# A two-layer mixer block and a gated block on one core: the opening, the start of layer 1 and the ends of layers re-ordered

## What is computed

```python
for l in range(2):
    mod = silu(c) @ w_ada[l] + b_ada[l]            # 3 x 1024: shift, scale, gate
    h = rms_norm(x, norm_g[l]) * (1.0 + scale) + shift
    proj = h @ w_in[l]                             # gq, gk, gv, glr, gz, dq, dk, dv, dz
    gqkv = silu(causal_depthwise_conv([gq, gk, gv], conv_w[l]))
    o_gla = gla_branch(...)                        # chunked gated linear attention, gate of rank 16
    o_diff = diff_branch(...)                      # block-causal attention; q and k normed by heads
    x = x + gate * ([o_gla, o_diff] @ w_out[l])
```

## Time and profile before

| | us |
|---|---|
| median of three runs | 1829.73 |
| lowest, highest | 1824.44, 1832.11 |
| the profiled execution's own time | 1827.28 |
| its span, from the first to the last instruction | 1825.5 |

### The profile page before, as it was taken

The page is one execution under the profiler, slowest core; times in us unless marked ns, Lnnn a source line. Parts: engine busy times, 40 slices in busy tenths (PEclk is TensorE's granted clock), DMA queues, the critical chain, the costliest instruction groups (busy, mean ns, idle before and its releaser), DMA issues.

```text
span 1825.5 us, 22633 instructions
## 1 busy us (share of the span) xinstructions
PE 1760.1 (96%) x9017; PEld 1447.4 (79%) x9017; DVE 939.9 (51%) x895; ACT 646.0 (35%) x801; POOL 661.9 (36%) x163
## 2 busy tenths in 40 slices
PE   5999999899999999999999999999999999999997
PEld 2677797688888788888888988888888788888885
DVE  4657657777665555554232346672223555554233
ACT  4332563344455433333333332232222433333221
POOL 2232233333222444443444444434444344443442
PEclk9999999899999999999999999999999999999998
DMA  8563112122111222322222332222222222232221
GB/s 335 208 237 108 47 64 74 51 86 74 47 70 47 88 96 92 103 103 70 96 95 87 115 115 92 92 92 92 92 92 92 83 102 92 97 110 71 95 95 62
DMA packets 29660, 180.79 MB, mean 99 GB/s; under 512 B 4342, under 2 KB 4476, under 8 KB 12060
## 3 DMA queue, kind: packets, MB, share of 16 engines
q1 hardware_dynamic: 24480, 161.50, 25.2%
q10 hardware_dynamic: 5116, 18.39, 2.8%
HBM read 177.78 MB, written 2.10 MB: 99 GB/s over the span
## 4 chain that ended last, share of the span: by engine, by line
issue 65%; PE 19%; POOL 15%; POOLq 0%; DVE 0%; ACT 0%; DVEq 0%; ACTq 0%
POOL wl L499 15%; PE ps L897 6%; PE ps L896 6%; PE ps L895 6%; DVE y L1441 0%; POOLq L504 0%; PE ps L1027 0%; POOLq L498 0%; ACT L600 0%; PE ps L1020 0%; DVE sq L1429 0%; DVEq L171 0%; ACT sq L572 0%; POOL glr L487 0%; ACTq L171 0%
## 5 line engine op out<-in xcount | busy, mean ns | idle before, releaser
L499 POOL TENSOR_TENSOR wl<-raw,wh 128x2048 fp32r<-128x2048 f32 (+1 forms) x152 | 659.9, 4342 | 1136.5 <-ACT wh L543 1136.5
L895 PE MATMUL ps<-xh,wh 128*128 128x512 f32 x1280 | 503.8, 394 | 12.9 <-DVE xl L1404 5.6
L896 PE MATMUL ps<-xl,wh 128*128 128x512 f32 x1280 | 499.4, 390 | 0.0
L897 PE MATMUL ps<-xh,wl 128*128 128x512 f32 x1280 | 499.4, 390 | 0.0
L543 ACT ACTIVATE wh<-raw 128x2048 fp32r<-128x2048 f32 x152 | 291.1, 1915 | 495.3 <-PE ps L897 457.7
L895 PEld LDWEIGHTS ps<-xh,wh 128*128 128x128 f32 x1280 | 240.9, 188 | 75.9 <-issue 24.3
L897 PEld LDWEIGHTS ps<-xh,wl 128*128 128x128 f32 x1280 | 240.8, 188 | 51.0
L896 PEld LDWEIGHTS ps<-xl,wh 128*128 128x128 f32 x1280 | 241.1, 188 | 48.9
L1802 DVE TENSOR_TENSOR fl<-tmp,fh 128x512 f32 x44 | 194.9, 4431 | 84.7 <-ACT fh L799 84.7
L927 PE MATMUL ps<-wh,xh 128*128 128x256 f32 x576 | 169.0, 293 | 1.5 <-POOL wl L499 1.5
L928 PE MATMUL ps<-wh,xl 128*128 128x256 f32 x576 | 163.6, 284 | 0.0
(11 more groups left out here) (241 smaller groups left out, 2160.5 us busy)
## 6 DMA issues: line engine op xcount, KB each, us to landing
raw<-ffn_in_stream SPq DMA_DIRECT2D x44, 1024.0 KB, 4.8
raw<-mixer_stream SPq DMA_DIRECT2D x40, 1024.0 KB, 4.8
raw<-layer_stream SPq DMA_DIRECT2D x36, 1024.0 KB, 4.9
raw<-ffn_out_stream SPq DMA_DIRECT2D x32, 704.0 KB, 4.1
ada_w<-w_ada SPq DMA_DIRECT2D x8, 1024.0 KB, 18.6
ada_late<-w_ada ACTq DMA_DIRECT2D x16, 512.0 KB, 5.2
ada_late<-w_ada ACTq DMA_DIRECT2D x8, 1024.0 KB, 6.9
x<-x_t SPq DMA_DIRECT2D x1, 2048.0 KB, 7.5
```

Source lines behind the costliest of these rows:

```text
L499: nc.gpsimd.tensor_tensor(wl[u][:, 0:size], raw[u][:, 0:size], wh[u][:, 0:size].bitcast(F32), ALU.subtract).then_inc(w_ready, 1)
L895: nc.tensor.matmul(bank_ap, w0, x0, start=first, stop=False)
L896: nc.tensor.matmul(bank_ap, w0, x1, start=False, stop=False)
L897: return nc.tensor.matmul(bank_ap, w1, x0, start=False, stop=last)
```

## The change

- **Opening.** The shift and scale weights of layer 0 come in four blocks of 256 features, all of the 1024 input rows at once (two loads a block, 1 KB a row). For each block PE makes 8 products, ScalarE copies the rows, PE turns them, and VectorE and ScalarE make the values of two feature tiles. Two steps of unit one stand behind the turns of blocks 1, 2 and 3 each, and the last two at the end. The two loads for the modulation are issued ahead of ScalarE's squares, six small loads behind the high part of chunk 0, and six more behind the high parts of block 1.
- **Layer 1.** Layer 0's output units now make raw halves of x times the modulation's gain. Unit one runs on them into banks 4 and 5. A product of the shift with the raw weights (8 fp32 products, 32 columns of weights) gives the shift's share, and 1/rms and that share are applied to the unit's output. The true values are made meanwhile and are used from unit two on, which runs step by step; `lr` stands behind it.
- **POOL** subtracts in two halves, each with its own count (`half_split`, `w_ready`), and PE waits for the half that it uses.
- **q's sums** are four products with 32 columns of weights, a copy and four transposes.
- **Ends.** `diff_ss` of the last block, `z_act` 1 and `diff_root` move ahead of the last parts, with the tables for root and Silu loaded by small instructions. The first output product waits for one bank. ScalarE takes the second chunk's high part ahead of the root in the late norms.
- `lr` moves from part 3 to part 4, the late tiles by one part.

The core of the diff (`first_steps` is the body of the old `first_feature_unit` for a range of steps; `half_ready` waits for `half_split` or `w_ready`; `ada_block` and `ada_turn` make the 8 products and the 4 transposes of a block):

```diff
-    put(3, "lr")
+    put(4, "lr")
...
-    put(33, "q_squares", (2, 3))
+    put(32, "q_squares", (2, 3))
+    put(33, "q_sums")
     put(33, "turn_keys", (0, 1))
-    put(34, "q_sums")
+    put(34, "q_turn")
...
-        if s >= 6 and s % 4 == 2:
+        if s >= 6 and s % 4 == 2 and s < STEPS:
...
+    put(52, "z_act", 1)
     for tb in range(TB):
         put(52, "gated_z", 0, tb)
-        put(53 + tb // 2, "mix", tb)
-    put(54, "diff_root")
-    put(54, "z_act", 1)
+    put(53, "diff_ss", 0)
+    put(53, "mix", 0)
+    put(53, "mix", 1)
+    put(53, "diff_root")
+    put(54, "mix", 2)
+    put(54, "mix", 3)
...
-            for k in range(KT):
-                sp.dma_start(ada_w[k][:], ins["w_ada"][0, k, :, 0:2 * D]).then_inc(ada_landed[k], 16)
-                if k in (0, 5):
-                    u = k // 5
+            for b in range(D // ADA_BLOCK):
+                for half in range(2):
+                    col = half * D + b * ADA_BLOCK
+                    sp.dma_start(ada_w[b][:, :, half * ADA_BLOCK:(half + 1) * ADA_BLOCK],
+                                 ins["w_ada"][0, :, :, col:col + ADA_BLOCK].rearrange("k p c -> p k c")
+                                 ).then_inc(ada_landed[b], 16)
+                if b in (0, 3):
+                    u = b // 3
                     sp.dma_start(raw[u][:], ins["layer0_stream"][u]).then_inc(raw_landed[u], 16)
 
...
+                for half in range(2):
+                    cols = slice(half * size // 2, (half + 1) * size // 2)
+                    last = nc.gpsimd.tensor_tensor(wl[u][:, cols], raw[u][:, cols], wh[u][:, cols].bitcast(F32),
+                                                   ALU.subtract)
+                    last.then_inc(half_split if half == 0 else w_ready, 1)
...
+                if n == 1:
+                    return first_unit_moved()
+                first = (0, CHUNK0["layer1"], CHUNK0["ffn1"], CHUNK0["mixer"], CHUNK0["ffn2"], CHUNKS)[n]
+                if not splits:
+                    take_high(first + 1)
...
+                    for b in range(D // ADA_BLOCK):
+                        act.wait_ge(ada_rows, b + 1)
+                        if b >= 2:
+                            act.wait_ge(ada_cols, b - 1)
+                        nc.scalar.activation(attn_t[:, b % 2], ps[:, 4 + b % 2], ACT.Copy).then_inc(rows_copied, 1)
+                        if b == 0:
+                            take_high(first)
+                            small_loads(0)
+                        if b == 3:
+                            take_high(first + 1)
+                        act.wait_ge(mod_ready, b + 1)
+                        for k in (2 * b, 2 * b + 1):
+                            act.wait_ge(xn_ready, k + 1)
+                            nc.scalar.activation(xh[:, k], xn[:, k], ACT.Identity, bias=mod[:, 0, k:k + 1],
+                                                 scale=mod[:, 0, 8 + k:9 + k]).then_inc(high_ready, 1)
+                        if b == 1:
+                            small_loads(1)
...
+                take_high(unit + 1)
+                nc.scalar.activation(spare[:, 0:1], eps[:, 0:1], ACT.Sqrt)
+                act.wait_ge(norm_ss, 2)
+                nc.scalar.activation(norm_sd[:], ps[:, 6, 0:TB], ACT.Sqrt, bias=eps[:, 0:1],
+                                     scale=1.0 / D).then_inc(norm_root, 1)
+                act.wait_ge(shift_rows, 1)
+                nc.scalar.activation(sq[:, 0, 0:256], ps[:, 2, 0:256], ACT.Copy).then_inc(shift_copied, 1)
+                act.wait_ge(norm_bc, 2)
+                nc.scalar.activation(sumsq[:], ps[:, 7], ACT.Copy).then_inc(spread_copied, 1)
+                for k in range(KT):
+                    if k == 2:
+                        for t in range(2):
+                            act.wait_ge(unit_scaled, t + 1)
+                            dst = u_in[:, t, CONV_K - 1:]
+                            nc.scalar.activation(dst, dst, ACT.Identity, bias=shift_sums[:, t:t + 1]
+                                                 ).then_inc(banks_free[0], 1)
+                    if k == 4:
+                        act.wait_ge(tile_done, 2 * unit + 2)
+                        take_high(unit + 2)
+                    act.wait_ge(tmp_ready, SPLIT0["norm1b"] + k + 1)
+                    link(nc.scalar.activation(tmp[:, k % 2], tmp[:, k % 2], ACT.Identity, bias=mod[:, 1, k:k + 1],
+                                              scale=mod[:, 1, 8 + k:9 + k]))
+                    act.wait_ge(unit_used, k + 1)
+                    nc.scalar.activation(xh[:, k], tmp[:, k % 2], ACT.Copy).then_inc(high_ready, 1)
...
+                    elif stage == "q_sums":
+                        act.wait_ge(q_rows, l + 1)
+                        nc.scalar.activation(sumsq[:], ps[:, 5], ACT.Copy).then_inc(q_copied, 1)
...
+                        nc.scalar.activation(spare[:, 0:1], eps[:, 0:1], ACT.Sqrt)
                         act.wait_ge(o_var, 2 * l + 2)
                         nc.scalar.activation(sd_o[:, 1], ss_o[:, 1], ACT.Sqrt, bias=eps[:, 0:1],
                                              scale=1.0 / P).then_inc(o_root, 1)
+                        nc.scalar.activation(spare[:, 1:2], eps[:, 0:1], ACT.Silu)
...
+            def first_moved_unit():
+
+                unit = UNIT0["layer1"]
+                claim(0, unit, 1)
+                chunk_ready(0, unit, 0)
+                raw_first = (xh, xl), SPLIT0["norm1"]
+                first_steps(*raw_first, range(0, 3), 0, 4, unit_used)
+                norm_sums(1)
+                first_steps(*raw_first, range(3, 4), 0, 4, unit_used)
+                pe.wait_ge(raw_landed[0], 16 * (unit // 2 + 1))
+                pe.wait_ge(late_mod, 2)
+                weights = raw[0][:].rearrange("p (t k c) -> p k t c", t=2, k=KT)
+                for r in range(KT // ADA_COLS):
+                    for g in range(ADA_COLS):
+                        k = r * ADA_COLS + g
+                        last = nc.tensor.matmul(ps[32 * g:32 * g + 32, 2, 0:256], c_wide[:, k], weights[:, k],
+                                                start=(r == 0), stop=(r == KT // ADA_COLS - 1))
+                last.then_inc(shift_rows, 1)
+                first_steps(*raw_first, range(4, 6), 0, 4, unit_used)
+                norm_spread(1)
+                pe.wait_ge(shift_copied, 1)
+                for t in range(2):
+                    last = nc.tensor.transpose(ps[:, 3, t * P:t * P + P], sq[:, 0, t * P:t * P + P], ident[:])
+                last.then_inc(shift_cols, 1)
+                first_steps(*raw_first, range(6, KT), 0, 4, unit_used)
+                pe.wait_ge(unit_used, KT)
+                pe.sem_inc(tile_done, 2)
...
+                    ada_turn(0)
...
+                    ada_block(1)
+                    ada_turn(1)
+                    claim(0, unit0, 0)
+                    chunk_ready(0, unit0, 0)
+                    first_steps((xh, xl), SPLIT0["norm0"], range(0, 2))
+                    for b in (2, 3):
+                        ada_block(b)
+                        ada_turn(b)
+                        first_steps((xh, xl), SPLIT0["norm0"], range(2 * b - 2, 2 * b))
+                    first_steps((xh, xl), SPLIT0["norm0"], range(KT - 2, KT))
...
+                    if l and (stage, j) == ("conv", 1):
                         if p == 0:
-                            first_feature_unit(unit0, unit0, (xh, xl), SPLIT0[f"norm{l}"])
+                            chunk_ready(0, unit, 0)
+                            claim(0, unit0, 0)
+                            first_steps((xh, xl), SPLIT0["norm1b"], range(KT), 1)
...
+                            last = nc.tensor.matmul(ps[32 * h:32 * h + 32, 5], inhalf[:], (sq, tmp)[h // 2][:, h % 2],
+                                                    start=True, stop=True)
+                        last.then_inc(q_rows, 1)
+                    elif stage == "q_turn":
+                        pe.wait_ge(q_copied, l + 1)
+                        for tb in range(TB):
+                            last = nc.tensor.transpose(ps[:, 4, tb * P:tb * P + P], sumsq[:, tb * P:tb * P + P], ident[:])
...
+                pe.wait_ge(banks_free[1], emptied(out_unit - 1, 0))
+                half_ready(0, out_unit, 0, 0)
+                first_out(0, 0, gla)
                 for u in range(2):
                     claim(0, out_unit, u)
-                chunk_ready(0, out_unit, 0)
-                gla = range(HEADS)
-                first_out(0, 0, gla)
+                half_ready(0, out_unit, 0, 1)
...
+                raw_done("norm1")
+                dve.wait_ge(shift_cols, 1)
+                link(nc.vector.tensor_reduce(shift_sums[:], ps[:, 3, 0:256].rearrange("p (t g r) -> p t g r", t=2, g=4)
+                                             [:, :, :, 0], AX_X, ALU.add))
+                dve.wait_ge(spread_copied, 1)
+                for k in range(KT):
+                    if k == 2:
+                        dve.wait_ge(tile_done, 2 * unit + 2)
```

(9 more changed lines are left out.)

211 lines of the change are left out of this document (124 added, 87 removed).

## The result

The changed kernel takes 1813.22 us, the median of five runs (1811.38 to 1816.03); its ratio to the kernel before is 0.9907, 95% interval 0.9891 to 0.9923, so some 17 us less. The profiled execution took 1816.03 us, the slowest of its five, while that of before lay 2.4 us under its median: the two spans differ by 11.2 us, the medians by more.

The account below looks back on a forecast made before the run. TensorE, busy 96% of the span, was taken as the bound, so time comes from its idle stretches, needless work and half clock. Terms: 5.1 + 5.5 + 1.7 + 2.3 + 4.5 + 4.0 + 3.4 + 0.5 - 4.0 = 23.0; 1804 us, range 1794 to 1818.

Parts of the forecast that it names:

- a new wait of over 3 us on a DMA: Anywhere in the new trace: one of the signs that the prediction said would show it wrong.
- Late norms, 5.1 us: Second unit after late norms: an earlier high part removes three waits on POOL's split, 1.8, 1.8 and 1.5 us.
- First output unit, 5.5 + 1.7: First output unit of a layer: two waits for the z copy go, 5.5 us, and layer 1's half clock, 1.7.
- Split in halves, 2.3 + 4.5: POOL's halves: 2.3 us at third output units, 4.5 in the attention from freeing VectorE, bounds 0 and 5.2.
- q's sums, 4.0 + 3.4: Sums of q's squares: fewer narrow products save 4.0 us; layer 1's clock staying full saves 3.4, bounds 0 and 3.4.
- The border, 0.5 gained: Layer 0 to layer 1: unit two's gain, less 3.6 us given back, nets 0.5; bounds 4 lost, 5 gained.
- The opening, 4.0 lost: Opening through low-rank part and unit two's first quarter: ends at 60.8 against 57.0; bounds 1.4 gained, 10 lost.
- Point (1): Opening: six small load issues on ScalarE take 2.9 us, delaying block 2's rows; TensorE stands from about 36.7 to 39.5.
- Point (2): Opening: block 3's parts wait behind chunk 1's high part (1.9) and POOL's first half (2.3); last steps start near 50.
- Point (3): Opening: lambda's exponent, about 3 us behind the last low part, stands before the emptying; unit two starts near 54.
- The rival of handed-on waits: Opening, layer 1's unit two, output units: waits and half clock merely move elsewhere, 1820 us; chance 0.12.
- 1 KB rows: Opening's modulation loads: 19% slower per byte expected; as a rival, loads set the opening, 1837 us at 130 ns; chance 0.06.

Follow-up runs that it names:

- e4: The changed kernel with POOL's subtraction in one instruction again and one count for it; ratio to the kernel before 0.9994, 15.9 us slower than the changed kernel.
- e12: The changed kernel with the second chunk's high part again behind the root before the late norms; ratio to the kernel before 0.9915, 1.5 us slower than the changed kernel.
- e11: The kernel before with only POOL's subtraction in halves and the two counts for it; ratio to the kernel before 0.9918.
- e7: The changed kernel with q's sums as before, 16 products two columns wide a layer; ratio to the kernel before 0.9965, 10.6 us slower than the changed kernel.
- e2: The changed kernel with the old border between layer 0 and layer 1; ratio to the kernel before 0.9878, 5.3 us faster than the changed kernel.
- e5: The changed kernel with three border edits: later claim, high part behind the loop, second tile emptied before the gate's passes; ratio to the kernel before 0.9851.
- e3: The changed kernel with old opening and old border, low-rank part and late modulation in their old places; ratio to the kernel before 0.9832.
- e1: The changed kernel with the old opening, low-rank part kept at its new place; ratio to the kernel before 0.9885, 4.0 us faster than the changed kernel.
- e6: The changed kernel with two opening edits: chunk 1's high part behind block 3's, two late loads issued after the last low part; ratio to the kernel before 0.9886.

## Why the prediction was right, and where its steps failed

The sign and the range held, with 6 us less gain than forecast. That is two large misses of the borders, about 10 us together, against some 4 us that the other terms gave beyond their sum. That they cancel in part is luck. One of the signs that the prediction named for being wrong came as well: a new wait of over 3 us on a DMA (the late tile, 4.3).

- **Late norms, 5.1 us.** The mechanism held: in e4, without the halves, the order leaves none of the three waits. What was missing is that the halves remove two of them as well, so beside the halves the order is worth only 1.5 (e12). The prediction counted each wait once, so the sum stands.
- **First output unit, 5.5 + 1.7.** Came: no wait on zg is left, and 565 to 580 us run at full clock. But the term hangs on the halves; without them 4.2 of it are handed to o_diff (e4).
- **Split in halves, 2.3 + 4.5.** Came in the trace; the upper side of the bounds was right: VectorE's instruction gets in between the halves. By the Trainium skill (SBUF — State Buffer, section "SBUF: two separate sides") the lock is held for an instruction; the trace now agrees with two POOL instructions back to back, 1.72 us in place of 3.91. Taken by themselves the halves are worth 15 us (e11) and not 6.8, in part because they also remove the two waits at the late norms, which the prediction gave to the order, and all 5.2 us of the attention's.
- **q's sums, 4.0 + 3.4.** The clock was right for the trace at hand; e7 has it in both layers, 6.7 us. The 10.6 us of e7 leave 3.9 for the products.
- **The border, 0.5 gained.** Failed; the changed border costs 5.3 us against the old one (e2). The claim was named and priced at 2.2; it took 3.3. The step that failed is the clock, for which the term has nothing: the longer claim and, more than it, half clock behind it make unit one late, so the spread starts at T + 17.4 (347.75, T = 330.4) and not at about T + 13.4, which follows from the prediction's own terms. The chain of unit two, priced at 18.9 us in all, is no longer than that: its last low part ends at T + 37.3, 18.9 us after the end of the spread. Two low parts were held up in it, by both of POOL's halves (1.59 and 2.16 us where 0.69 is usual), 2.4 us together, which is what the prediction put there. Then TensorE does the last steps at half clock (365 to 370 us), and unit two ends at T + 41, not at T + 33 to T + 35.5. The give-back at the gate was there, 2.2 to 3.8 us for ScalarE's copy. e5, with the claim later, the high part behind the chain and the copy ahead of the gate, has 94.0 us for the whole border.
- **The opening, 4.0 lost.** Failed in size. The term runs to the end of the low-rank part and the first quarter of unit two; TensorE is through with them at 66.2 (70.45 less its wait) in place of 57.2, so 9 us are lost in the trace, and 8.4 by the times (e2 to e3). That e1 gives 4.0 is chance: it leaves the low-rank part at its new place. Up to the decay of layer 0 TensorE idles 29.4 us in place of 23.8 (stretches of over 0.25 us), 5.6 of the 10.1 us that this stretch grows by; half clock, for which this term too has nothing, comes on top. Point (1), six issues in 2.9 us, didn't bind: the issues were over at 34.6, and block 2's rows were copied at 37.94, 0.7 us of wait as for any such copy. Point (2) was right in kind, but POOL's second half stood in the way too: the last steps start at 51.94 and not near 50, after 3.9 us of idle. Point (3) bound nothing as it stood and 5.2 us once the wait ahead of it was gone (e6). The late tile was expected about 4 us later; its load is issued 9 us later (54.18 to 63.15), 2.7 us before TensorE asks for it, and it starts 11.3 us later.
- **The clock.** This is what both borders have in common. The rival of handed-on waits was partly true: the stretches above show half clock behind the new waits. Its time (1820 us) didn't come, since 3.4 + 1.7 and the 5.5 of the output units did. By the Trainium skill (TensorE: Matmul & The Clock Gate, section "Part 1: The HAM clock gate") idle time brings the clock down; e1 and e11, below, show that nearly the same idle time may or may not.
- **1 KB rows.** Slower by about what the prediction worked out. From 14 to 36 us the queue moved 7.60 MB in place of 8.64, and from 15 to 35 us the rates are 326 to 371 GB/s in place of 403 to 422, 18% more time a byte at the mean where 19% were worked out:

```profile
q1 hardware_dynamic: 6515, 7.60, 105.9%
```

That a load lands 13.0 us after its issue in the median (18.6 before) is no gain: the issues themselves now take up to 5.0 us each, so the later loads are issued later. TensorE waits for them once, 15.3 us for block 0, which is 2 MB where the first row block of before was 1 MB. What the rows cost in time no run shows, since none changed them alone.

## What to carry to other kernels

When one engine's long instruction shuts out another, cutting it in two can be worth as much as a whole reordering (15 us here), and it changes what the reordering is worth: try it alone and first. When a chain is moved into a stretch that used to be idle, count each half of each long instruction that can start within it and a stretch at half clock behind each new wait, and put what only later work needs (the next chunk's high part, an exponent, a second claim) behind the chain. Take waits away one after the other until the next one in line shows itself; the estimate of a single one says little.

## What the runs showed of the hardware that was not expected

**The clock behind nearly the same idle time.** Five kernels have the old opening, with a wait of 2.4 us ahead of unit one. From 40 to 45 us, in the trace of before and then in that of e3:

```profile
40.00:45.00 5.00, 5.00 (x24) 1.00 0.04 16
```

```profile
40.00:45.00 5.00, 5.00 (x13) 0.50 0.07 28
```

In e3 the waits between 30 and 42 us are longer (5.5 us in four, against 4.3 in three before). But e1 shows 0.66 there with waits of 4.6 us, and e11 1.00 with 4.4, in the same three places. So the same program part runs at full clock in one profile and partly at half in another, a difference of 2 to 3 us. Two single profiles can differ by that at each wait, and a border is to be judged by timed runs. Why it falls in one and not in the other stays open.

**Narrow products can lower the clock of a busy engine.** In e7 the clock fell to 0.50 at the 16 products two columns wide while TensorE had not idled; with four products of 512 columns in their place it stays at 1.00. It fell in four of the six places where the profiles have the narrow ones.

**One instruction gets in.** In the opening VectorE waits while POOL has two instructions back to back; one of its instructions passes between them, and the next waits for the second: 3.07 us for two that take 1.00, then 3.42 for two that take 1.33, beside POOL's 4.92. At the border a low part passes in the same way, then a product that reads one operand from a result bank takes its usual 0.69 us beside POOL's second half (361.97), and only the next low part is held up again (2.16).
